# Another order for the first projection's matrix products, and three small loads on another DMA queue, in a two-layer encoder kernel

## The chip, the cores and the metric

The kernel runs on one core of a Trainium2 chip (trn2). The metric is the device time of one execution, in microseconds (us), taken as the median of several runs. The engines are called PE (TensorE: matrix products, transposes), DVE (VectorE), ACT (ScalarE), POOL (GpSimd) and SP (SyncE, which here only starts transfers). "ACTq" and "SPq" are the instruction queues of ACT and SP when they start a transfer.

## What is computed

The reference is a two-layer encoder on one sequence of 256 tokens and 1024 channels. Only the first steps of the first layer matter here:

```python
def _rmsnorm(x, g):
    x32 = x.astype(jnp.float32)
    inv = lax.rsqrt(jnp.mean(x32 * x32, axis=-1, keepdims=True) + EPS)
    return (x32 * inv).astype(x.dtype) * g

def _swiglu(h, w_in, w_out):
    gu = h @ w_in
    gate, up = jnp.split(gu, 2, axis=-1)
    return (jax.nn.silu(gate) * up) @ w_out

def reference(x, ...):
    for l in range(DEPTH):
        x = x + 0.5 * _swiglu(_rmsnorm(x, ffn1_norm[l]), ffn1_w_in[l], ffn1_w_out[l])
        # the mixer: p = h @ w_mix_in, spatial gating and windowed attention, @ w_mix_out
        x = x + 0.5 * _swiglu(_rmsnorm(x, ffn2_norm[l]), ffn2_w_in[l], ffn2_w_out[l])
    return x
```

`w_in` is 1024 x 5632 (gate and up halves of 2816 columns), `w_out` 2816 x 1024, all float32. `rel_bias` (32 x 8 numbers) becomes the attention's position bias, needed in the mixer.

## The kernel before, in words

**Products in three parts.** Every float32 operand is split into a rounded part "hi" (float32r) and the rest "lo" = original - hi. A product of two operands is the sum of three PE products: hi*hi, hi*lo and lo*hi. For weights ACT writes `w_hi` with a copy and DVE writes `w_lo` with a subtraction. For the input, PE transposes a token tile of 128 rows into PSUM (`TR`), DVE multiplies it with the norm's gain into `sc` (`take_xg`), ACT rounds that into `xT_hi` and DVE subtracts into `xT_lo`. The 1/rms of each token is applied later, to the result.

**Weights as a stream of units.** A unit is 128 x 2048 numbers (1 MB). SP loads units in their order of use into three buffers `raw`; `w_hi` and `w_lo` have six slots each. Unit n+3 is loaded when DVE has made `w_lo` of unit n (semaphore `lo_ready`). Position 0 and 1 of the first feed-forward block hold 256 gate and 256 up columns (chunk 0) for input channels 0-511 and 512-1023; positions 2 and 3 are chunk 1's gate and up columns, 4 is the 256 rows of `w_out` for chunk 0, 5 and 6 are chunk 2's, 7 is chunk 1's rows, and so on through 11 chunks. Units 0 and 1 come in two halves each (`load_first`), which ACT and DVE split half by half (`split_first`, `split_rest`), so that PE can start early.

**Order of work.** There is no scheduler: each engine's program is one list written out by hand, and semaphores hold an instruction back until what it needs is there. An engine works strictly in its own order. The opening of layer 0 goes like this:

- PE: 6 warm-up products, the transpose of the first norm's gains, transposes of token tile 0 (`transpose_x(0, 0, 0)`), 12 more warm-up products (`warm_up`, all on the identity matrix, their results unused). Then `ffn(0, 0)`: `enter(0, 0)` (12 products of tile 0 with unit 0), transposes of tile 1, `enter(0, 1)`, `enter(1, 0)`, `enter(1, 1)` (12 products each). `enter` waits for `xT_lo` of its half and calls `project`, which waits for the lower part of the unit's first half (`half_lo`) before any product, and for the whole unit (`split_ready`) before its second half. Each k tile then has its three products in a row (`products`, L1123, L1124, L1126).
- After that PE waits for `h_done`: the gated activation of tile 0 (`mul_rows`, DVE L782, on ACT's `silu_rows`, L513), then computes chunk 1's gate columns (`enter_T(1, 0, 0)`, L1186 and L1194), transposes the activations of both tiles (`transpose_h`, L1176), and goes on with `enter_T(1, 0, 1)`, `enter_T(1, 1, 0)`, which waits for `hT_lo` of tile 0 (L788), `other_rows()` (L1394 to L1398: it transposes the rest of the small parameter rows and waits for their loads, `rows_loaded` and `head_rows_loaded`), `enter_T(1, 1, 1)` and `leave(0, t)`.
- ACT: the halves of units 0 and 1, rounding of tile 0, two sums of squares (L551), rounding of tile 1 (`take_xT(0, 0, 1)`, L556). Then it starts three small loads (`rb`, L699; two sets of 16 rows of norm gains, L701), stores the two 1/rms vectors to DRAM (`store_inverse`, L562, which waits for POOL's result `inv_done`), splits unit 2, does `silu_rows` of tile 0, splits unit 3, `silu_rows` of tile 1, splits unit 4, reads the 1/rms back spread over partitions (L567), and rounds the transposed activations (`take_hT`, L535).
- DVE: the subtractions for units 0 and 1 between the input's, then `w_lo` of unit 2, `mul_rows` of tile 0, `w_lo` of unit 3, `mul_rows` of tile 1, `take_hT` (L788) for both tiles, `w_lo` of unit 4.
- POOL: 1/rms of both tiles (`inverse_rms`, L431 and L432), three loads of small rows (q and k gains, L446; `sgu_b`, L448), then the table `brow`, built from `rb` with 31 copies (L454), its store to DRAM (L459) and, spread over the next chunks, 8 loads of `bias` (L465).

## Time and profile before

| What | Value |
|---|---|
| median of 3 runs | 909.88 us (909.81 to 909.89) |
| the profiled execution | 909.78 us |
| its span in the profile | 908.0 us |
| PE busy | 901.9 us (99%) |
| PE weight loads | 767.2 us (84%) |
| DVE, ACT, POOL busy | 610.8, 483.0, 48.1 us |
| HBM traffic | 184 GB/s over the span |
| granted PE clock, every slice | 9 (90% or more) in tenths |

The profiled execution is 0.10 us under the median of the runs, and 1.8 us of it lie outside the profiled span. Times in rows are microseconds from the start of the span. A PE product is drawn until its result is out, so its length overlaps the next one; the step from one start to the next is what it takes from PE.

### The profile page before, as it was taken

To read this page: it belongs to the slowest core of one execution; us is meant where nothing else is said; L and a number is where in the kernel's file an instruction comes from. 1 tells how busy PE (TensorE), PEld (TensorE's weight loads), DVE (VectorE), ACT (ScalarE), POOL (GpSimd) and SP (SyncE) were. 2 spreads that over 40 slices of the span, in tenths; PEclk is the share of its full clock that TensorE was granted. 3 is DMA by queue.
4 is the path that set the end of the run, shared out by engine and by line. 5 is a ranking of instruction groups with operands and counts; after the bars stand their busy time and mean duration, and the time that the engine had idled before them with its cause. 6 is when DMAs were issued, how large, how long until landed. Compare 5 with 4: busy or idle time off the path is not lost.

```text
span 908.0 us, 13716 instructions
## 1 busy us (share of the span) xinstructions
PE 901.9 (99%) x4902; PEld 767.2 (84%) x4902; DVE 610.8 (67%) x791; ACT 483.0 (53%) x604; POOL 48.1 (5%) x105
## 2 busy tenths in 40 slices
PE   8999999999999999999999999999999999999998
PEld 7888888887788888888888888888877888888887
DVE  5576666687966765665776666666789567566564
ACT  6455455467845554544555545535678355454551
POOL 2200001012100000000010000000210100000000
PEclk9999999999999999999999999999999999999999
DMA  8776666654174656455547555554531656645531
GB/s 280 237 221 206 218 205 201 226 169 139 51 261 131 215 185 220 151 200 214 164 158 249 182 201 188 185 214 157 186 139 47 232 157 221 230 146 204 205 139 46
DMA packets 120909, 167.53 MB, mean 185 GB/s; under 512 B 7101, under 2 KB 100097, under 8 KB 120873
## 3 DMA queue, kind: packets, MB, share of 16 engines
q1 hardware_dynamic: 117536, 163.47, 53.2%
q0 software_dynamic: 1104, 2.90, 1.4%
q10 hardware_dynamic: 2232, 0.69, 0.4%
q8 instruction: 22, 0.36, 0.2%
q14 instruction: 15, 0.11, 0.0%
HBM read 165.71 MB, written 1.31 MB: 184 GB/s over the span
## 4 chain that ended last, share of the span: by engine, by line
PE 92%; DVE 5%; ACT 1%; DMA 1%; issue 1%; SPq 0%; ACTq 0%; DVEq 0%
PE TR L1186 16%; PE U L1186 16%; PE TR L1194 8%; PE U L1194 8%; PE C L1123 6%; PE C L1126 6%; PE C L1124 6%; PE D L1126 5%; PE D L1123 5%; PE D L1124 5%; PE U L1123 2%; PE U L1126 2%; PE U L1124 2%; DVE sc L982 1%; DVE w_lo L766 1%; PE TR L1163 1%
## 5 line engine op out<-in xcount | busy, mean ns | idle before, releaser
L766 DVE TENSOR_TENSOR w_lo<-raw,w_hi 128x2048 fp32r<-128x2048 f32 x150 | 340.1, 2289 | 109.2 <-ACT w_hi L494 109.1
L494 ACT ACTIVATE w_hi<-raw 128x2048 fp32r<-128x2048 f32 x150 | 282.2, 1905 | 20.3 <-DMA raw<-in_ffn_w_in_dram 12.9
L1186 PE MATMUL U<-xT,w_hi 128*128 128x512 f32 x640 | 167.4, 392 | 0.3 <-DVE small L782 0.3
L1186 PE MATMUL TR<-xT,w_hi 128*128 128x512 f32 x640 | 165.9, 391 | 0.0
L1186 PEld LDWEIGHTS TR<-xT,w_hi 128*128 128x128 f32 x640 | 119.2, 188 | 21.5
L1186 PEld LDWEIGHTS U<-xT,w_hi 128*128 128x128 f32 x640 | 115.1, 189 | 20.2 <-DVE small L782 0.7
L518 ACT ACTIVATE small<-U 128x512 f32<-128x512 f32 x40 | 23.9, 598 | 151.8 <-PE U L1186 151.7
L1194 PEld LDWEIGHTS U<-xT,w_lo 128*128 128x128 f32 x640 | 86.9, 189 | 6.5
L1194 PEld LDWEIGHTS TR<-xT,w_lo 128*128 128x128 f32 x640 | 87.6, 190 | 4.3
L1194 PE MATMUL TR<-xT,w_lo 128*128 128x256 f32 x640 | 89.4, 282 | 0.0
L1194 PE MATMUL U<-xT,w_lo 128*128 128x256 f32 x640 | 88.7, 281 | 0.0
L540 ACT ACTIVATE hT_hi<-small 128x256 fp32r<-128x256 f32 x80 | 33.1, 418 | 89.2 <-DVE small L812 89.2
L793 DVE TENSOR_TENSOR small<-U,small 128x512 f32<-128x512 f32 x40 | 27.6, 690 | 71.1 <-ACT small L518 70.9
L1123 PE MATMUL D<-w_hi,hT_hi 128*128 128x512 f32 x176 | 68.7, 390 | 0.0
L1124 PE MATMUL D<-w_lo,hT_hi 128*128 128x512 f32 x176 | 68.5, 389 | 0.0
L1123 PE MATMUL C<-w_hi,hT_hi 128*128 128x512 f32 x176 | 68.5, 389 | 0.0
L1124 PE MATMUL C<-w_lo,hT_hi 128*128 128x512 f32 x176 | 68.5, 389 | 0.0
L805 DVE TENSOR_TENSOR small<-TR,small 128x256 f32<-128x256 f32 x80 | 33.7, 421 | 43.0 <-ACT small L527 42.8
L531 ACT ACTIVATE small<-small 128x512 f32<-128x512 f32 x40 | 25.3, 632 | 67.8 <-DVE small L800 67.8
L1126 PE MATMUL D<-w_hi,hT_lo 128*128 128x512 f32 x176 | 55.5, 389 | 0.0
L1123 PE MATMUL U<-w_hi,xT 128*128 128x512 f32 (+1 forms) x144 | 54.8, 381 | 0.4 <-DVE xT L857 0.4
L1126 PE MATMUL C<-w_hi,hT_lo 128*128 128x512 f32 x176 | 54.2, 389 | 0.0
(140 smaller groups left out, 1110.8 us busy)
## 6 DMA issues: line engine op xcount, KB each, us to landing
raw<-in_ffn_w_in_dram SPq DMA_DIRECT2D x168, 512.0 KB, 4.7
raw<-in_ffn_w_out_dram SPq DMA_DIRECT2D x88, 512.0 KB, 4.1
raw<-in_w_mix_in_dram SPq DMA_DIRECT2D x28, 512.0 KB, 4.3
raw<-in_w_mix_out_dram SPq DMA_DIRECT2D x16, 512.0 KB, 3.7
raw<-in_ffn_w_in_dram SPq DMA_DIRECT2D x16, 256.0 KB, 4.4
bias<-bias_rows POOLq DMA_DIRECT2D x8, 192.0 KB, 5.4
xs<-in_x_dram SPq DMA_DIRECT2D x2, 512.0 KB, 4.9
out_dram<-xs SPq DMA_DIRECT2D x3, 256.0 KB, 2.1
```

What stands on the lines that cost most here:

```text
L494: act.activation(w_hi[:, p % SLOTS, :], raw[:, p % RAW, :], ACT.Copy).then_inc(hi_ready, 1)
L518: act.activation(gate, U_pair[:, :, S:2 * S], ACT.Copy).then_inc(gate_copied, 1)
L531: act.activation(gate, gate, ACT.Silu).then_inc(silu_done, 1)
L540: act.activation(hT_hi[:, c % 2, kk, :], h[:, kk, :], ACT.Copy).then_inc(hT_hi_done, 1)
L766: dve.tensor_tensor(w_lo[:, p % SLOTS, :], raw[:, p % RAW, :], w_hi[:, p % SLOTS, :].bitcast(F32), ALU.subtract).then_inc(lo_ready, 1)
L793: dve.tensor_tensor(gate, U_pair[:, :, 0:S], gate, ALU.add).then_inc(gate_added, 1)
L805: dve.tensor_tensor(h[:, kk, :], TR[kk][:, 0:S], h[:, kk, :], ALU.add).then_inc(up_added, 1)
L1123: pe.matmul(out_, x_hi, w_hi[:, slot, c], start=start, stop=False)
L1124: pe.matmul(out_, x_hi, w_lo[:, slot, c], start=False, stop=False)
L1126: last = pe.matmul(out_, x_lo, w_hi[:, slot, c], start=False, stop=stop)
L1186: last = pe.matmul(to, w_hi[:, slot, cols_of(k, kk)], xT[:, k, :, :], start=k == 0, stop=k == KT - 1)
L1194: last = pe.matmul(to[:, 0:S], w_lo[:, slot, cols_of(k, kk)], xT_hi[:, k, :], start=False, stop=False)
```

## The change

PE's first four groups of products in layer 0 are written out in a function of their own, `enter_first`. It waits for each part of the operands by itself and issues the products that need only that part: hi*hi as soon as the rounded parts are there, then hi*lo or lo*hi. Tile 0's transposes of the next tile stand after 16 of its products instead of 12. The products are the same 48, added into the same PSUM banks. All other projections, and the same place in layer 1, are as before. The loads of `rel_bias` and of 2 x 16 rows of norm gains leave ACT's list and stand in POOL's, after the two `inverse_rms` and ahead of POOL's own three small loads.

```diff
@@ POOL @@
             inverse_rms(0, 0, 0)
             inverse_rms(0, 0, 1)
+            with nc.allow_non_contiguous_dma(reason="256 numbers, once"):
+                pool.dma_start(rb[:, :], rel_bias.rearrange("b h -> h b")).then_inc(rb_loaded, 16)
+            for r0, v in ((16, mix_norm), (32, ffn2_norm)):
+                pool.dma_start(rows[r0:r0 + 2 * KT, :], v.rearrange("l (k p) -> (l k) p", p=P)).then_inc(rows_loaded, 16)
             for r0, v in ((48, q_norm), (50, k_norm)):
@@ ACT @@
             for L in range(DEPTH):
                 take_xT(L, 0, 1)
-                if L == 0:
-                    with nc.allow_non_contiguous_dma(reason="256 numbers, once"):
-                        act.dma_start(rb[:, :], rel_bias.rearrange("b h -> h b")).then_inc(rb_loaded, 16)
-                    for r0, v in ((16, mix_norm), (32, ffn2_norm)):
-                        act.dma_start(rows[r0:r0 + 2 * KT, :], v.rearrange("l (k p) -> (l k) p", p=P)).then_inc(rows_loaded, 16)
                 ffn(L, 0, [POS_KV, POS_Q, POS_Q + 1])
@@ PE @@
+            def enter_first():
+
+                def product(t, k, w_of):
+                    kk = k % 4
+                    return pe.matmul(U[t][:, :], xT_hi[:, k, t * P:(t + 1) * P], w_of[:, k // 4, kk * 512:(kk + 1) * 512],
+                                     start=k == 0 and w_of is w_hi, stop=False)
...
+                pe.wait_ge(half_hi, 1)
+                pe.wait_ge(xT_hi_done, n_tran(0, 0, 0, 0))
+                high_high(0, (0, 1))
+                pe.wait_ge(half_lo, 1)
+                high_low(0, (0, 1))
+                pe.wait_ge(xT_lo_done, n_tran(0, 0, 0, 0))
+                low_high(0, (0, 1))
+                pe.wait_ge(hi_ready, n_unit(0, 0))
+                high_high(0, (2, 3))
+                low_high(0, (2, 3))
+                split_ready(0, 0)
+                high_low(0, (2, 3))
+                pe.wait_ge(half_hi, 2)
+                pe.wait_ge(xT_hi_done, n_tran(0, 0, 0, 1))
+                high_high(0, (4, 5))
+                pe.wait_ge(xT_lo_done, n_tran(0, 0, 0, 1))
+                low_high(0, (4, 5))
+                pe.wait_ge(x_loaded[1], 16)
+                transpose_x(0, 0, 1)
+                pe.wait_ge(half_lo, 2)
+                high_low(0, (4, 5))
+                pe.wait_ge(hi_ready, n_unit(0, 1))
+                high_high(0, (6, 7))
+                split_ready(0, 1)
+                high_low(0, (6, 7))
+                low_high(0, (6, 7), True).then_inc(gu_ready, 1)
+                for u in range(2):
+                    ks = range(4 * u, 4 * u + 4)
+                    pe.wait_ge(xT_hi_done, n_tran(0, 0, 1, u))
+                    high_high(1, ks)
+                    high_low(1, ks)
+                    pe.wait_ge(xT_lo_done, n_tran(0, 0, 1, u))
+                    low_high(1, ks, True).then_inc(units_used, 1)
...
-                enter(0, 0)
-
-                if f == 1:
-                    pe.wait_ge(x_new, n_x_new(L, 1, 1, 1))
+                if L == 0 and f == 0:
+                    enter_first()
                 else:
-                    pe.wait_ge(x_loaded[1], 16)
-                    pe.wait_ge(x_new, n_x_new(L, -1, 1, 1))
-                pe.wait_ge(xg_done, n_tran(L, 2 * f, 0, 1))
-                transpose_x(L, 2 * f, 1)
-                enter(0, 1)
-                enter(1, 0)
-                enter(1, 1)
+                    enter(0, 0)
+
+                    pe.wait_ge(x_new, n_x_new(L, 2 * f - 1, 1, 1))
+                    pe.wait_ge(xg_done, n_tran(L, 2 * f, 0, 1))
+                    transpose_x(L, 2 * f, 1)
+                    enter(0, 1)
+                    enter(1, 0)
+                    enter(1, 1)
```

PE's list from the second warm-up to the transposes of tile 1, before the change. In brackets stand the semaphores that an instruction waits for; L1123 is hi*hi, L1124 the product with `w_lo`, L1126 the one with `xT_lo`. A row that only repeats the one ahead of it is left out here and in the next list.

```order
L1391 MATMUL C1<-ident 128x128 x12
L1123 MATMUL U<-w_hi,xT 128x512 [waits half_lo,xT_lo_done]
L1124 MATMUL U<-w_lo,xT 128x512
L1126 MATMUL U<-w_hi,xT 128x512
...
L1123 MATMUL U<-w_hi,xT 128x512 [waits lo_ready]
...
L1163 MATMUL TR<-ident,xs 128x128 [waits xg_done,x_new,x_loaded1]
```

The same place after the change (L1169 is now a product with `xT_hi`, L1183 the one with `xT_lo`).

```order
L1446 MATMUL C1<-ident 128x128 x12
L1169 MATMUL U<-w_hi,xT 128x512 [waits xT_hi_done,half_hi]
L1169 MATMUL U<-w_lo,xT 128x512 [waits half_lo]
L1183 MATMUL U<-w_hi,xT 128x512 [waits xT_lo_done]
L1169 MATMUL U<-w_hi,xT 128x512 [waits hi_ready]
L1183 MATMUL U<-w_hi,xT 128x512 x2
L1169 MATMUL U<-w_lo,xT 128x512 [waits lo_ready]
L1169 MATMUL U<-w_hi,xT 128x512 [waits xT_hi_done,half_hi]
L1183 MATMUL U<-w_hi,xT 128x512 [waits xT_lo_done]
L1162 MATMUL TR<-ident,xs 128x128 [waits x_loaded1]
```

The first product waited for both lower parts; now it waits for the two rounded parts, and the lower parts are waited for one by one, with two products behind each wait.

ACT's list from the rounding of tile 1 to `silu_rows` of tile 0, before:

```order
L556 ACTIVATE xT<-sc 128x4x128 [waits xg_done] x2
L699 DMA rb<-in_rel_bias_dram 8x32x1
L701 DMA wsT<-in_mix_norm_dram 16x128
L701 DMA wsT<-in_ffn_norm_dram 16x128
L562 DMA inv_rows<-inv 128x1 [waits inv_done]
L562 DMA inv_rows<-inv 128x1
L494 ACTIVATE w_hi<-raw 128x2048 [waits units_used,unit_loaded2]
L513 ACT_TABLE_LOAD [waits inv_done]
L513 ACTIVATE small<-U,inv 128x256 [waits gu_ready]
```

and after:

```order
L560 ACTIVATE xT<-sc 128x4x128 [waits xg_done] x2
L566 DMA inv_rows<-inv 128x1 [waits inv_done]
L566 DMA inv_rows<-inv 128x1
L498 ACTIVATE w_hi<-raw 128x2048 [waits units_used,unit_loaded2]
L517 ACT_TABLE_LOAD [waits inv_done]
L517 ACTIVATE small<-U,inv 128x256 [waits gu_ready]
```

The three loads are gone from ACT's list, and the stores of the 1/rms follow the rounding at once. POOL's list at the place where they now stand:

```order
L431 TENSOR_SCALAR mean<-ms 128x1 [waits ms_done]
L432 TENSOR_TENSOR inv<-mean,mhalf 128x1 [waits pool_step]
L446 DMA rb<-in_rel_bias_dram 8x32x1
L448 DMA wsT<-in_mix_norm_dram 16x128
L448 DMA wsT<-in_ffn_norm_dram 16x128
L450 DMA wsT<-in_q_norm_dram 2x2x64
L450 DMA wsT<-in_k_norm_dram 2x2x64
L452 DMA wsT<-in_sgu_b_dram 8x128
L454 MEMSET brow 8x511
L458 COPY brow<-rb 8x38 [waits rb_loaded,pool_step]
```

The q, k and `sgu_b` loads stood directly behind `inverse_rms` and now have the three moved ones ahead of them.

## Rows read from the trace of the kernel before

**Rows 1.** The page, busy time of the engines over the whole span.

```profile
PE 901.9 (99%) x4902; PEld 767.2 (84%) x4902; DVE 610.8 (67%) x791; ACT 483.0 (53%) x604; POOL 48.1 (5%) x105
```

**Rows 2.** Waits of PE, whole span: us in total, times, longest.

```profile
PE C L1391 <- POOL mhalf L426: 1.7, 1, 1.7
PE U L1123 <- DVE xT L857: 0.4, 1, 0.4
PE TR L1176 <- DVE small L782: 0.3, 1, 0.3
PE U L1186 <- DVE small L782: 0.3, 1, 0.3
```

**Rows 3.** Timeline of PE, 4 to 31.3 us: start, length, instruction, [idle before <- releaser].

```profile
5.66 2.84 PE L1391 MATMUL C<-ident 128*128 128x128 f32 x24
8.93 0.50 PE L1123 MATMUL U<-w_hi,xT 128*128 128x512 f32 x1 [0.42 <-DVE xT L857]
...
11.83 1.09 PE L1163 MATMUL TR<-ident,xs 128*128 128x128 f32 x8
12.67 0.47 PE L1123 MATMUL U<-w_hi,xT 128*128 128x512 f32 x1
...
20.74 0.39 PE L1126 MATMUL U<-w_hi,xT 128*128 128x512 f32 x1
21.42 0.50 PE L1186 MATMUL U<-xT,w_hi 128*128 128x512 f32 x1 [0.30 <-DVE small L782]
...
28.10 0.39 PE L1186 MATMUL TR<-xT,w_hi 128*128 128x512 f32 x1
...
30.99 0.27 PE L1398 MATMUL C<-ident,wsT 60*128 60x60 f32 x1
```

**Rows 4.** Timeline of DVE, 4 to 32 us, same columns.

```profile
11.91 1.22 DVE L776 TENSOR_TENSOR w_lo<-raw,w_hi 128x1024 fp32r<-128x1024 f32 x1
...
18.74 2.29 DVE L766 TENSOR_TENSOR w_lo<-raw,w_hi 128x2048 fp32r<-128x2048 f32 x1 [3.02 <-ACT w_hi L494]
20.95 0.42 DVE L782 SCALAR_TENSOR_TENSOR small<-U,small 128x256 f32<-128x256 f32 x1
...
27.10 0.76 DVE L788 TENSOR_TENSOR hT_lo<-TR,hT_hi 128x256 fp32r<-128x256 f32 x2 [2.13 <-ACT hT_hi L535]
```

**Rows 5.** Timeline of ACT, 5 to 45 us, same columns.

```profile
6.92 1.14 ACT L556 ACTIVATE xT<-sc 128x512 fp32r<-128x512 f32 x2
...
13.77 1.23 ACT L556 ACTIVATE xT<-sc 128x512 fp32r<-128x512 f32 x2
14.37 0.54 ACTq L699 DMA_DIRECT2D rb<-in_rel_bias_dram  x1
...
15.77 0.92 ACTq L562 DMA_DIRECT2D inv_rows<-inv  x2
16.79 1.92 ACT L494 ACTIVATE w_hi<-raw 128x2048 fp32r<-128x2048 f32 x1 [1.79 <-issue]
...
24.78 1.91 ACT L494 ACTIVATE w_hi<-raw 128x2048 fp32r<-128x2048 f32 x1 [2.12 <-DMA raw<-in_ffn_w_out_dram]
...
26.68 0.66 ACT L535 ACTIVATE hT_hi<-TR 128x256 fp32r<-128x256 f32 x2
```

**Rows 6.** Timeline of POOL, 14 to 41 us, same columns.

```profile
14.31 0.55 POOL L432 TENSOR_TENSOR inv<-mean,mhalf 128x1 f32<-128x1 f32 x1
14.81 0.77 POOL L446 DMA_DIRECT2D wsT<-in_q_norm_dram  x1
...
16.16 0.56 POOL L448 DMA_DIRECT2D wsT<-in_sgu_b_dram  x1
```

**Rows 7.** DMA issues in a window: count, KB each, median us from issue to landing.

```profile
raw<-in_ffn_w_in_dram SPq DMA_DIRECT2D x2, 512.0 KB, 6.5
...
raw<-in_ffn_w_out_dram SPq DMA_DIRECT2D x2, 512.0 KB, 8.5
...
wsT<-in_sgu_b_dram POOLq DMA_DIRECT2D x1, 4.0 KB, 9.0
```

More of the change, by code:

```diff
@@ L1164, in transpose_x, with high_high, high_low, low_high @@
                     last.then_inc(xT_psum, 1)
+            def enter_first():
[3 more added lines that the diff above has]
+                                     start=k == 0 and w_of is w_hi, stop=False)
+                def high_high(t, ks):
+                    for k in ks:
+                        product(t, k, w_hi)
+                def high_low(t, ks):
+                    for k in ks:
+                        last = product(t, k, w_lo)
+                    return last
+                def low_high(t, ks, stop=False):
+                    for k in ks:
+                        last = pe.matmul(U[t][:, :], xT_lo[:, k, t * P:(t + 1) * P],
+                                         w_hi[:, k // 4, (k % 4) * 512:(k % 4 + 1) * 512],
+                                         start=False, stop=stop and k == KT - 1)
+                    return last
+                pe.wait_ge(half_hi, 1)
[31 more added lines that the diff above has]
+                    low_high(1, ks, True).then_inc(units_used, 1)
```

## The prediction

> **What bounds the kernel now.** I read the page first: PE is busy 901.9 of 908.0 us [rows 1], so what the end can move by is what PE waits, plus what its own work costs. The list of PE's waits for the whole span comes next, and it has four entries only [rows 2]: 1.7 us before the first warm-up, and three of 0.4, 0.3 and 0.3 us, all of which stand in the first 26 us. Behind them PE works without a wait to the end. Two things follow. A microsecond won in the opening stays won, for nothing later would take it up. And the ceiling is low: the change touches no later place. Then I read the timelines of the four engines side by side in the opening.
>
> PE's warm-up products end near 8.35 (24 of them from 5.66, each step about 0.12 us), yet the first real product starts at 8.93, released by DVE's `xT_lo` [rows 3]. From 12.67 to 20.74 stand 36 products, 35 steps and so (8.07)/35 = 0.23 us each; the transposes of tile 1 take 12.67 - 11.83 = 0.84 us. PE is through with the 48 products at 20.74 + 0.23 = 20.97, and then the next product starts at 21.42, released by DVE's `mul_rows` [rows 3].
>
> That second wait hangs on a chain that starts on ACT. Its rounding of tile 1 ends at 15.00; it starts the first small load at 14.37 and the stores of 1/rms at 15.77, for 0.92 us, so that unit 2's rounding begins only at 16.79, behind an idle time of 1.79 us whose releaser is "issue" [rows 5]. DVE's `w_lo` of unit 2 begins at 18.74 (idle 3.02 us for ACT) and takes 2.29 us, `mul_rows` stands behind it from 20.95 to 21.37 [rows 4], and PE starts at 21.42. So the three loads are on the path to 21.42, though ACT is busy only half of the span.
>
> **The change, part by part.**
>
> *PE's new order.* Rounded parts: `xT_hi` of the first half is there by 6.92 + 0.57 = 7.49, before the warm-ups end at 8.35 [rows 3, 5]. DVE makes the first half of `w_lo` ahead of `xT_lo`, whose end released PE at 8.93; so the products with `w_lo`, wanted two products later at 8.4 + 0.46 = 8.86, wait 0.07 us at most, and those with `xT_lo`, wanted at 9.3, not at all. So PE should run from about 8.4 without a stall: 48 x 0.23 + 0.84 + about 0.2 for the first start = 12.1, done at 8.35 + 12.1 = 20.4 instead of 20.97. The second unit's last subtraction ends at 13.13 [rows 4], and its two products with `w_lo` come as numbers 21 and 22, at 8.4 + 20 x 0.23 + 0.84 = 13.8, so that wait is covered, with 0.7 us over. Transposes of tile 1 move from 11.83 to 8.4 + 16 x 0.23 = 12.1, which costs nothing, since DVE takes their results only when it is done with `w_lo` at 13.13. PE gains 0.57 us here. By itself this is worth nothing: the next thing PE waits for is `mul_rows` at 21.37, which does not use PE's last products, so PE would arrive earlier and wait longer.
>
> *The loads off ACT.* They fill 15.77 - 14.37 = 1.40 us of ACT's queue [rows 5]. Not all of it comes back, as the stores behind them wait for POOL's second 1/rms, which ends at 14.31 + 0.55 = 14.86 [rows 6]. So the stores start at 14.93 instead of 15.77: gain 0.84 us. Unit 2's rounding then starts at 15.95; its `w_lo` at 17.90, `mul_rows` ends at 20.53, and PE goes on at 20.58 instead of 21.42. PE itself is ready at 20.4, just in time. Units 2 and 3 must be in `raw` by then: unit 3 was issued up to 11.27 and landed after 6.5 us in the median [rows 7], at 17.8, and it is wanted at 20.39 - 0.84 = 19.55. The second short wait (0.3 us, for `mul_rows` of tile 1) hangs on the same chain and moves with it. Without the new order, PE would come at 20.97 and the loads alone would give 21.37 - 20.97 = 0.3 to 0.4 us. So the parts belong together: order 0, loads about 0.4, both 0.84.
>
> *The next wait.* PE comes to `enter_T(1, 1, 0)` at 28.10 - 0.84 = 27.26 [rows 3]. It needs `hT_lo` of tile 0, whose subtraction ran from 27.10, 0.38 us for the first of the two, so until 27.48 [rows 4]; that was after ACT's `take_hT` at 26.68, which stood behind unit 4's rounding, and this began at 24.78, released by the landing of `w_out` [rows 5]. The landing does not move with ACT. If it stays, PE waits 27.53 - 27.26 = 0.27 us, plus 0.1 us for starting afresh (the first product after the stall, at 8.93, is 0.50 us long and that at 20.74 0.39 [rows 3]), and the gain is 0.5 us. If it comes only 0.3 us sooner, the gain is the whole 0.84 us. `w_out`'s two halves took 8.5 us in the median from issues at 13.2 and 13.7 [rows 7], hence one of them took about 11 us to 24.7. I take it that the landing comes somewhat earlier, since the 1/rms stores start earlier and no longer have `rb`'s 256 numbers ahead of them on their queue; no row shows this, so the two ends are 0.84 and, if it comes 0.5 us later, 0.
>
> *The loads on POOL.* An issue there takes 0.56 to 0.77 us [rows 6]: three add 1.7 to 2.3 us. `sgu_b`, the last, was issued at 16.16 and landed 9.0 us later, at 25.2 [rows 7]; now 27.5 at most, with the same 9.0 us. PE wants it at 30.99 - 0.84 = 30.15 in `other_rows()` [rows 3]: 2.6 us of cover. The price of an issue with 256 separate numbers is not in the trace on POOL; ACT took 0.54 us for it [rows 5]. It lies between 0.5 us and the 2.6 us of cover more than the rest before it costs anything. `brow` and `bias` are wanted chunks later, so their delay costs nothing. POOL's own next duty, the 1/rms of the next block, comes far later.
>
> Sum: -0.84 from both parts, 0 to +0.35 from the landing of `w_out`; I take -0.8. On the profiled execution that is 909.78 - 0.8 = 908.98, and the median lies 0.10 above it: **909.1 us**.
>
> **The rivals.**
>
> *A, the `w_out` landing takes the place of the removed wait.* As above, -0.5 us if it stays, less if it comes later: 909.4 to 909.9. For it: ACT's row at 24.78 already names this transfer as releaser after 2.12 us idle. Against: only 0.3 us earlier are enough. The Trainium skill speaks for it ("DMA: Bandwidth & Descriptors", Queues, rings and completion order): each DMA engine serves the queue rows that have work in turn, so loads on POOL's row beside those of SP and ACT would take turns from the weights. By it the landing would come later and the gain would go towards 0. No row here shows which queue an engine served.
>
> *B, slower: the small rows come late and PE stalls in `other_rows()`.* POOL's issue at 14.81 ran beside a DVE subtraction and took 0.77 us, the one at 16.16 with DVE idle took 0.56 us [rows 6]. If DVE can hold POOL for a whole subtraction, the last issues meet `w_lo` of unit 2 (17.90 to 20.2) and that of unit 3 (21.5 to 23.8), and `sgu_b` is issued at 23.8 and lands 9.0 us later at 32.8, where PE wanted it at 30.15: 2.65 us of stall and 0.1 for starting afresh against 0.84 of gain, 909.88 + 1.91 = 911.8 us. It decides from an issue later than 30.15 - 9.0 = 21.15. Against it: 0.2 us is all that the two rows differ by. The Trainium skill has the rule ("SBUF — State Buffer", SBUF: two separate sides): while DVE works in its two-port mode POOL cannot write descriptors, and a POOL transfer of about 620 ns took about 3100 ns. The trace bears it out only in the 0.2 us.
>
> *C, more than forecast.* Were the stores not held by POOL's 1/rms, the chain would gain the 1.40 us, and PE, ready at 20.4, would use 1.0 of it: 908.8 us.
>
> *D, nothing.* ACT's issue goes as late as before, for a reason the profile does not show, or `w_out` lands 0.5 us later: 909.8 us.
>
> **How the numbers follow.** Forecast (gain 0.7 to 0.9) 0.45; A 0.30; C 0.07; D 0.12; B 0.05; something unforeseen of over 2 us gain 0.01. The range 908.6 to 910.0 holds the forecast, A, C and D, all but B and the tails. A difference of 0.2% is 1.8 us, about what a measurement of this kernel can tell from no change. All cases but B lie within it: same 0.93, slower 0.05, faster 0.02.
>
> **What would show it.** First product near 8.4 and no DVE releaser before it; products in steps of 0.23 us until the transposes near 12.1; PE done with 48 products near 20.4; stores of 1/rms issued from 14.93; unit 2's rounding at 15.95; PE's next product at 20.58. Then at 27.3 either no idle time (forecast) or one of 0.3 us with DVE's `hT_lo` as releaser (A). An idle time on PE before L1398's successor with a DMA as releaser would be B. I am wrong if PE has a new wait anywhere behind 31 us, or if the stores start as late as 15.8.

## The result, and the profile after

| | before | after |
|---|---|---|
| median of 22 runs each | 909.88 us | 910.77 us |
| lowest to highest | 909.62 to 910.60 | 909.50 to 913.14 |
| profiled execution, its span | 909.78, 908.0 us | 910.46, 908.7 us |

The ratio is 1.0014 (95% interval 1.0008 to 1.0020): slower by 0.14%, 0.9 us in the medians, where I forecast 909.1 us. Both the sign and the range were wrong. The change's runs fall into two groups: 14 from 909.50 to 910.96 us with a mean granted clock of 1.000, and 8 from 912.40 to 913.14 us with 0.998. The profiled execution is from the first group. The 14 runs alone have a median of 910.4 us, 0.5 over before; the rest of the 0.9 comes from the runs with 0.998.

First the page's busy times of the changed kernel and its list of PE's waits (us in total, times, longest), against [rows 1, 2].

```profile
PE 901.9 (99%) x4902; PEld 767.3 (84%) x4902; DVE 611.2 (67%) x791; ACT 482.8 (53%) x604; POOL 49.8 (5%) x108
```

```profile
PE C L1446 <- POOL mhalf L426: 1.7, 1, 1.7
PE TR L1242 <- DVE hT_lo L787: 1.4, 1, 1.4
PE TR L1232 <- DVE small L781: 0.3, 1, 0.3
```

PE's own work is the same to a tenth. The wait for `xT_lo` and that for `mul_rows` of tile 0 are gone, as forecast; in their place stands one of 1.4 us for `hT_lo`. PE's timeline in the opening, against [rows 3]:

```profile
5.85 2.84 PE L1446 MATMUL C<-ident 128*128 128x128 f32 x24
8.45 0.71 PE L1169 MATMUL U<-w_hi,xT 128*128 128x512 f32 x2
...
12.18 1.03 PE L1162 MATMUL TR<-ident,xs 128*128 128x128 f32 x8
...
19.43 1.07 PE L1183 MATMUL U<-w_hi,xT 128*128 128x512 f32 x4
20.40 0.50 PE L1242 MATMUL U<-xT,w_hi 128*128 128x512 f32 x1
...
28.64 0.50 PE L1242 MATMUL TR<-xT,w_hi 128*128 128x512 f32 x1 [1.42 <-DVE hT_lo L787]
...
31.64 0.27 PE L1453 MATMUL C<-ident,wsT 60*128 60x60 f32 x1
```

At 20.40 the change leads by 21.42 - 20.40 = 1.02 us. At 28.64 it trails by 28.64 - 28.10 = 0.54, at L1453 by 31.64 - 30.99 = 0.65, and at the end of the span by 0.7. From L1453 to the end both kernels take 877.0 to 877.1 us (908.7 - 31.64, 908.0 - 30.99), so this one instruction's start tells what a kernel is worth; I use it below. All is won and lost ahead of 28.64. ACT's timeline says by what, against [rows 5]:

```profile
13.69 1.14 ACT L560 ACTIVATE xT<-sc 128x512 fp32r<-128x512 f32 x2
14.84 0.83 ACTq L566 DMA_DIRECT2D inv_rows<-inv  x2
15.77 1.92 ACT L498 ACTIVATE w_hi<-raw 128x2048 fp32r<-128x2048 f32 x1 [0.95 <-POOL inv L432]
...
25.95 1.91 ACT L498 ACTIVATE w_hi<-raw 128x2048 fp32r<-128x2048 f32 x1 [4.31 <-DMA raw<-in_ffn_w_out_dram]
...
27.77 0.64 ACT L539 ACTIVATE hT_hi<-TR 128x256 fp32r<-128x256 f32 x2
```

ACT is 1.0 us ahead at its unit 2 (15.77 against 16.79) and has nothing to do from 21.6: it waits 4.31 us for `w_out`, which it sees landed at 25.95, not at 24.78. `take_hT` then runs at 27.77 (26.68 before), DVE's subtraction at 28.16 (27.10 before, [rows 4]), and PE, which arrives at 28.64 - 1.42 = 27.22, stands still. `w_out` was issued no later (SP's timeline: from 12.97, before from 13.2). What did the DMA engines do meanwhile? The busy times by stretch; of the last three columns the first is PE's granted clock, the second the DMA engines' busy share, the third GB/s.

```profile
20.00:22.00 2.00, 2.00 (x14) 1.59 (x13) 1.04 (x3) 1.64 (x2) 0.00 (x0) 1.00 0.57 27
22.00:24.00 2.00, 1.71 (x10) 1.16 (x8) 1.94 (x2) 0.00 (x0) 0.00 (x0) 1.00 0.08 3
24.00:26.00 2.00, 2.00 (x14) 1.87 (x15) 0.00 (x0) 0.05 (x1) 0.12 (x1) 1.00 0.26 44
```

From 22 to 24 us they moved 3 GB/s. In the trace's list of packets the last 4 KB packet of `w_out` ends at 20.24, and the last one of ACT's stores at 20.35. Each half of a load raises its semaphore in sixteen steps, one for each part. Of the second half of `w_out` three parts were reported by 21.27 and the other thirteen between 23.87 and 25.92; before the change 14 were reported by 21.42, one at 22.28 and one at 24.75. So the report came up to 5.7 us after the last packet. The loads behind it were held up too: the pair of `w_in` halves that SP started at 20.26 and 20.85 had only landed at 32.19. POOL's side, against [rows 6, 7], first its timeline and then the DMA issues (median us to landing):

```profile
14.25 0.56 POOL L432 TENSOR_TENSOR inv<-mean,mhalf 128x1 f32<-128x1 f32 x1
14.75 0.90 POOL L446 DMA_DIRECT2D rb<-in_rel_bias_dram  x1
...
17.81 0.55 POOL L452 DMA_DIRECT2D wsT<-in_sgu_b_dram  x1
...
25.88 6.11 POOL L458 COPY brow<-rb 8x38 f32<-8x38 f32 x31 [7.01 <-DMA rb<-in_rel_bias_dram]
```

```profile
inv_rows<-inv ACTq DMA_DIRECT2D x2, 0.5 KB, 11.0
rb<-in_rel_bias_dram POOLq DMA_DIRECT2D x1, 1.0 KB, 11.0
...
wsT<-in_sgu_b_dram POOLq DMA_DIRECT2D x1, 4.0 KB, 9.9
```

`sgu_b` landed at 17.81 + 9.9 = 27.7, wanted at 31.64: no cost. POOL sees `rb` at 25.88 as ACT sees `w_out` at 25.95: several transfers of different queues are reported at about the same time.

### The profile page after: what moved, and what is told of

It is laid out like the page before. It is cut to its first block, busy times and chain, and to the rows that moved or that the text cites. A ratio compares the mean times of both kernels' runs of the same rounds, so it can differ in the third digit from the quotient of the medians.

```text
span 908.7 us, 13713 instructions
## 1 busy us (share of the span) xinstructions
PE 901.9 (99%) x4902; PEld 767.3 (84%) x4902; DVE 611.2 (67%) x791; ACT 482.8 (53%) x604; POOL 49.8 (5%) x108
## 4 chain that ended last, share of the span: by engine, by line
PE 92%; DVE 5%; DMA 2%; ACT 1%; issue 0%; SPq 0%; DVEq 0%
PE TR L1242 16%; PE U L1242 16%; PE TR L1250 8%; PE U L1250 8%; PE C L1122 6%; PE C L1125 6%; PE C L1123 6%; PE D L1125 5%; PE D L1122 5%; PE D L1123 5%; PE U L1122 2%; PE U L1125 2%; PE U L1123 2%; DVE sc L981 1%; DMA raw<-in_ffn_w_out_dram 1%; DVE w_lo L765 1%
## 5 line engine op out<-in xcount | busy, mean ns | idle before, releaser
L792 DVE TENSOR_TENSOR small<-U,small 128x512 f32<-128x512 f32 x40 | 27.7, 691 | 73.3 <-ACT small L522 73.0
L1123 PE MATMUL D<-w_lo,hT_hi 128*128 128x512 f32 x176 | 68.5, 389 | 0.0
L1123 PE MATMUL C<-w_lo,hT_hi 128*128 128x512 f32 x176 | 68.5, 389 | 0.0
L1122 PE MATMUL U<-w_hi,xT 128*128 128x512 f32 (+1 forms) x128 | 48.4, 378 | 0.0
```

Of the source, the lines that this page charges most:

```text
L792: dve.tensor_tensor(gate, U_pair[:, :, 0:S], gate, ALU.add).then_inc(gate_added, 1)
L1122: pe.matmul(out_, x_hi, w_hi[:, slot, c], start=start, stop=False)
L1123: pe.matmul(out_, x_hi, w_lo[:, slot, c], start=False, stop=False)
```

## The experiments

Three things could hold back `w_out`'s completion. **Theory 1:** `rb`'s 256 single numbers, now on POOL's queue beside `w_out`. **Theory 2:** the two 1/rms stores of 128 single numbers each (`inv_rows`), which start 0.9 us earlier than before and so meet more of `w_out`. **Theory 3:** POOL's loads in flight, whatever they are made of. The kernel before, run again beside each set, took 909.91, 910.00, 909.92 and 909.92 us. "Landing" is the start of ACT's rounding of `w_out`; where ACT came later than the data, it is an upper end.

**The parts apart.** `e1_order_only`: the three loads go back to ACT.

```diff
-                pool.dma_start(rb[:, :], ...)      # and the two loads of rows
+                    act.dma_start(rb[:, :], ...)   # behind take_xT(0, 0, 1), as before
```

> The new order of the products alone; the three loads stay on ACT's list. The trace of the change shows PE's new order as forecast and then a wait of 1.42 us at 27.2 for hT_lo, behind a landing of w_out at 25.9 instead of 24.7. All theories on that landing put its cause in the small transfers, so here it stays near 24.7: PE is ready at 20.4 and waits for mul_rows until 21.4 as before, and the time is that of before, 909.9 us within 0.15. If the new order itself moved the landing, the time would be over 910.3 us.

Measured: 910.43 us (910.27 to 910.80, 11 runs), ratio 1.0003 [0.9994, 1.0013], 0.5 more than expected. PE in its trace:

```profile
4.78 1.97 PE L1163 MATMUL TR<-ident,xs 128*128 128x128 f32 x8
...
12.97 1.03 PE L1163 MATMUL TR<-ident,xs 128*128 128x128 f32 x8
```

The first transposes took 1.97 us, in the change 1.23 and before 1.09. The trace's record of the granted clock says why: it shows full speed, the 2.4 GHz level, from 6.69 us on here, from 5.11 in the change and from 4.62 before. The 128x128 products ahead of that moment start 0.21 us apart, those behind it 0.11. (The view by stretches prints 1.00 even ahead of it, because the record starts only there.) So the transposes of tile 1 come at 12.97, and DVE, which I had counted as busy to 13.13, has waited 0.39 us for them. To see whether this is chance, the same kernel once more:

> The kernel with the new order alone once more, for a second trace. Its first took 910.43 us in the median, 0.5 over before, and its trace shows PE's clock at 1.2 GHz until 6.69 us (4.62 before), so that warm-ups, products and tile 1's transposes come 0.8 us late and DVE waits 0.39 us for them at 13.6, ACT 0.56 at 14.3. Theory W (the new order has no slack against late warm-ups): where the clock rises near 5 us, DVE does not wait and the time is 909.9; where it rises past 6 us it is 910.4. Theory P (the transposes after 16 products instead of 12 delay DVE in any case): DVE waits at 13 us whatever the clock does.

It gave 910.04 us in one run, with full speed from 6.21, the first transposes at 1.76 us and no wait on DVE: between the theories, and it settles nothing. (e13 below has full speed from 6.23 and DVE's wait again, 0.35 us.) `e9_transposes_after_14` takes the cover back instead: order only, tile 1's transposes two products earlier.

```diff
                 high_high(0, (4, 5))
-                pe.wait_ge(xT_lo_done, n_tran(0, 0, 0, 1))
-                low_high(0, (4, 5))
                 pe.wait_ge(x_loaded[1], 16)
                 transpose_x(0, 0, 1)
+                pe.wait_ge(xT_lo_done, n_tran(0, 0, 0, 1))
+                low_high(0, (4, 5))
```

> The new order alone, with tile 1's transposes two products earlier (after 14 instead of 16), just when x has landed (11.7 to 11.8 us). Theory P or W: the transposes, and with them DVE's and ACT's rounding of tile 1 and everything behind it up to mul_rows, come up to 0.45 us earlier than in the new order alone, so 910.0 to 910.1 us instead of 910.43. If the 0.5 us have another cause: 910.4 us still.

Measured: 909.98 us (909.66 to 910.32), 1.0001 [0.9992, 1.0010], as expected. The intervals of the two ratios overlap, but only one of the 11 runs here is above the lowest of e1. The reading that fits is that "later transposes cost nothing" had too little slack: where PE's clock rises late, the order-only kernel pays, about 0.45 us between the two medians. It isn't shown closer than that, for in e9's own trace the clock was up at 4.77. I didn't try this edit on the full change.

`e2_loads_only`: the loads on POOL, PE's order as before (`enter_first` taken out).

> The loads on POOL alone; the products in their old order. Theories 1 to 3 (the small transfers delay w_out's landing): landing near 25.9, PE waits for hT_lo until 28.6, end as in the full change, 910.4 to 910.9 us, with some runs 2 us slower. Theory 4 (the landing only varied by chance in the profiled execution): about 0.3 us faster than before, 909.6 us.

Measured: 912.94 us (910.44 to 914.55), 1.0027 [1.0018, 1.0036]; 7 of 11 runs had a mean granted clock of 0.998 or less, which puts the median 2 us over what I expected. So the loads' part carries the loss. ACT and PE in its trace:

```profile
14.86 0.84 ACTq L566 DMA_DIRECT2D inv_rows<-inv  x2
...
27.24 1.91 ACT L498 ACTIVATE w_hi<-raw 128x2048 fp32r<-128x2048 f32 x1 [5.57 <-DMA raw<-in_ffn_w_out_dram]
```

```profile
29.93 0.50 PE L1185 MATMUL TR<-xT,w_hi 128*128 128x512 f32 x1 [2.67 <-DVE hT_lo L787]
```

With the stores as early as in the change, PE stalls 2.67 us.

**Theories 1 and 3.** `e3_rb_in_8_pieces`: the full change, `rb` read in 8 runs of 128 bytes instead of 256 single numbers (which leaves wrong entries in the bias table).

```diff
-                pool.dma_start(rb[:, :], rel_bias.rearrange("b h -> h b")).then_inc(rb_loaded, 16)
+                pool.dma_start(rb[:, :], rel_bias.rearrange("(a b) h -> a (b h)", a=NH)).then_inc(rb_loaded, 16)
```

> The full change, but rel_bias is read in 8 contiguous runs of 128 bytes instead of 256 single numbers, so that the bias table holds wrong entries. Theory 1 (the 256 single-number writes of rb, now on a queue of their own beside the 256 of the 1/rms stores, hold up the completions): w_out lands at 24.7 or earlier, PE's wait at 27.2 shrinks to 0.3 us or nothing, time 909.0 to 909.4 us. Theory 2 (the 1/rms stores, started 0.9 us earlier, stand ahead of w_out's last completions) and theory 3 (three more loads on POOL's queue, whatever their shape): no change, 910.4 to 910.9 us.

Measured: 911.19 us (910.05 to 912.95), 1.0014 [1.0005, 1.0023], the same as the change; landing at 26.73. Theory 1 falls. The profiled execution is one with clock 0.998 and shows where the other two microseconds come from. PE, and the stretches around the stall:

```profile
29.43 0.72 PE L1242 MATMUL TR<-xT,w_hi 128*128 128x512 f32 x1 [2.20 <-DVE hT_lo L787]
...
33.96 0.27 PE L1453 MATMUL C<-ident,wsT 60*128 60x60 f32 x1
```

```profile
26.00:28.00 2.00, 1.23 (x6) 0.68 (x4) 0.00 (x0) 1.27 (x1) 1.70 (x13) 1.00 0.69 55
28.00:30.00 2.00, 0.57 (x2) 0.48 (x3) 1.05 (x3) 1.67 (x4) 0.40 (x1) 0.88 0.48 128
30.00:32.00 2.00, 2.00 (x10) 1.99 (x9) 2.00 (x2) 0.00 (x0) 0.00 (x0) 0.50 1.07 379
32.00:34.00 2.00, 2.00 (x8) 1.28 (x6) 0.50 (x1) 0.00 (x0) 0.00 (x0) 0.76 1.01 347
```

PE stood still for 2.20 us up to 29.43; then its granted clock fell to 0.50, the 1.2 GHz level, and the same work up to L1453 took 33.96 - 29.43 = 4.53 us where the change's trace has 31.64 - 28.64 = 3.00. That is 1.5 us more, beside the stall itself, and 911.0 - 34.0 = 877.0 us remain as always.

`e5_small_loads_first`: all six small loads of POOL right behind the constants, so that none is in flight with `w_out`.

```diff
             pool.memset(mhalf[:, :], -0.5).then_inc(consts_ready, 1)
+            # rb, mix_norm, ffn2_norm, q_norm, k_norm, sgu_b
...
             inverse_rms(0, 0, 1)
-            # rb, mix_norm, ffn2_norm, q_norm, k_norm, sgu_b
```

> The full change, but all six small loads stand first in POOL's list, right after the constants, so that none is in flight when w_out lands; the 1/rms stores stay where the change has them. Theory 2 (the stores of 256 single numbers to DRAM hold up w_out's completion): the landing stays at 25 to 27 us, time 910.3 to 912.5 us. Theory 3 (the loads on POOL's queue hold it up): landing by 22.3, PE does not wait at 27.2, time 909.0 us or, with the chain on ACT shortened no further, 908.9.

Measured: 911.33 us (910.97 to 913.46), 1.0015 [1.0006, 1.0024]. ACT:

```profile
10.09 1.06 ACT L504 ACTIVATE w_hi<-raw 128x1024 fp32r<-128x1024 f32 x1 [7.55 <-DMA raw<-in_ffn_w_in_dram]
...
19.05 0.83 ACTq L566 DMA_DIRECT2D inv_rows<-inv  x2
...
27.45 1.92 ACT L498 ACTIVATE w_hi<-raw 128x2048 fp32r<-128x2048 f32 x1 [1.54 <-DMA raw<-in_ffn_w_out_dram]
```

The small loads, single numbers among them, now meet the first weights, and those are seen at 10.09 instead of 5.71; PE waits 3.2 us there. `w_out`, issued 4.4 us later than in the change (17.35), lands 10.1 us after its issue, against 13.0 in the change and 8.6 in e4 below; 15 of the 16 parts of its second half were reported by 22.78. So a delay is there without POOL's loads, but a smaller one, and the upset opening makes the comparison a weak one. It takes e12 to decide on theory 3.

**Theory 2, the stores.** `e4_inv_store_late`: the full change; in the first block the stores stand behind the rounding of `w_out`, and the reading back behind it.

```diff
-                store_inverse(L, f)
+                if not first:                  # first: layer 0, block 0
+                    store_inverse(L, f)
                 split(L, pos_in(f, 1, 0))
...
                 split(L, pos_out(f, 0))
-                spread_inverse(L, f)
+                if first:
+                    store_inverse(L, f)
+                else:
+                    spread_inverse(L, f)
...
                 copy_up(L, f, 1, 1)
+                if first:
+                    spread_inverse(L, f)
```

> The full change, but in the first block of layer 0 the two stores of 1/rms (256 single numbers to DRAM) start only after unit 4's rounding, and the spreading load correspondingly later. Theory 2: w_out lands by 22.3, where 15 of its 16 parts were in the run before, so PE does not wait at 27.2; time 909.0 us. ACT's rounding of unit 2 also comes 0.9 us earlier, but PE is ready only at 20.4, which gives 0.2 us more at most. Theory 1: rb's 256 numbers still delay the landing to 24.5 or later, 909.3 to 910.5 us. The late spreading load could make DVE's scale_gate wait near 42, which PE does not feel until 50.

Measured: **908.22 us** (907.83 to 909.27), 0.9982 [0.9973, 0.9991], better than expected. ACT:

```profile
14.93 1.90 ACT L498 ACTIVATE w_hi<-raw 128x2048 fp32r<-128x2048 f32 x1
...
21.87 1.92 ACT L498 ACTIVATE w_hi<-raw 128x2048 fp32r<-128x2048 f32 x1 [0.84 <-DMA raw<-in_ffn_w_out_dram]
21.87 0.83 ACTq L566 DMA_DIRECT2D inv_rows<-inv  x2
```

`w_out` lands at 21.87 instead of 25.95, with all six loads on POOL still there: theory 2 holds. PE's only wait left is the one before the warm-up. What I had underrated is the second effect: the stores' issue (0.83 us) leaves ACT's path too, unit 2's rounding begins at 14.93, and the 0.3 us for `mul_rows` of tile 1 goes as well.

The slow stretch has moved as well. The stretches of e4's trace, same columns as before:

```profile
22.00:24.00 2.00, 2.00 (x13) 1.70 (x12) 1.08 (x2) 2.00 (x3) 2.00 (x11) 1.00 1.01 330
24.00:26.00 2.00, 2.00 (x14) 1.78 (x13) 1.91 (x3) 0.33 (x2) 2.00 (x8) 1.00 1.30 51
```

The stores' packets now end at 24.36, and from there to 30 us the DMA engines move 51 to 58 GB/s, with two `w_in` halves started at 22.99 and 23.55 in the queue, which have landed only at 34.90. The pair ahead of them, started at 19.40 and 19.99, had landed at 24.72. In e8 below, with its stores at 21.97, the stretches from 26 to 34 us are the slow ones (35 to 73 GB/s). So the stores still hold up what is in flight behind them, for some 6 to 8 us; here that is a load that nothing waits for.

Is it then the change or the stores? `e6_before_inv_store_late` has the same edit on the kernel before.

> The kernel before, with nothing of the change, but with the first block's 1/rms stores moved behind unit 4's rounding. It tells what the change is worth when the landing is out of the way. The stores' 0.9 us leave ACT's path, so mul_rows of tile 0 ends near 20.5 and PE, ready at 20.97 in the old order, does not wait: 0.4 us, and 0.3 us for the second wait: 909.1 to 909.3 us by theory 2. The kernel with the change and the late stores took 908.22 us, so the change would be worth about 0.9 us there. If the late stores were worth nothing without the change: 909.9 us.

Measured: 908.98 us (908.80 to 910.08), 0.9989 [0.9981, 0.9998]. The kernel before paid for the early stores too, 0.9 to 1.0 us, and once they are late the change is worth 908.98 - 908.22 = 0.76 us, close to the 0.84 that I had worked out. (The intervals of the two ratios overlap; 9 of e4's 11 runs lie below the lowest of e6.) And its parts? `e11_order_and_late_stores` is e4 with the three loads back on ACT.

> New order and late stores, the three small loads left on ACT. With late stores alone 908.98 us, with the full change and late stores 908.22 us. In the trace with late stores alone mul_rows of tile 0 ends at 20.50 and PE's old order ends at 21.0: PE bounds. So the order should bring what there was (PE ready near 20.3, mul_rows at 20.5): 908.4 to 908.5 us; moving the loads on top is worth 0.2 us only. If the moved loads carry the 0.76 us: 908.9 us.

Measured: 909.68 us (908.97 to 910.65), 0.9995 [0.9986, 1.0004]; expected 1.2 us less. PE's waits in its trace:

```profile
PE C L1454 <- POOL mhalf L426: 1.7, 1, 1.7
PE U L1177 <- ACT xT L556: 0.7, 1, 0.7
PE TR L1240 <- DVE small L789: 0.3, 1, 0.3
PE U L1250 <- DVE small L789: 0.3, 1, 0.3
```

With the loads on ACT the waits for `mul_rows` are back; the 0.7 us is a first weight that came late in this execution, the slowest of the 11. ACT takes that weight up at 7.82 us against 6.03 in e6's trace, so I compare the rows less 1.8: PE takes up chunk 1 at 20.5 (22.33 less 1.8) against 20.97 in e6, then waits for `mul_rows` of tile 1 and gets past it at 24.3 (26.11 less 1.8) against 24.35. So the second `mul_rows`, which my expectation left out, takes the gain back. Even the lowest of 11 runs, 908.97, is no better than the median of late stores alone, 908.98: the order alone is worth nothing here either. Why the median is 0.7 us worse is open; the late first weight is seen in one trace only.

What about the stores does it? `e7_stores_after_silu`: the full change with the stores one step later in ACT's list, behind `silu_rows` of tile 0, and the reading back as late as in e4.

> The full change with the 1/rms stores at another time: started behind silu_rows of tile 0, near 18.3 us, instead of 14.84 or 21.87, the spreading load late as in the run with late stores. Theory 2 with the time of the stores as what counts (their numbers must not come before w_out's last parts, which move until 20): landing 21 to 23, 908.2 to 908.9 us. If any store that starts before the landing delays it: landing 24 or later, 909.5 to 911 us.

Measured: 911.26 us (909.27 to 914.32, 12 runs), 1.0014 [1.0003, 1.0025]. ACT:

```profile
15.02 1.90 ACT L498 ACTIVATE w_hi<-raw 128x2048 fp32r<-128x2048 f32 x1
15.17 0.84 ACTq L566 DMA_DIRECT2D inv_rows<-inv  x2
...
25.64 1.91 ACT L498 ACTIVATE w_hi<-raw 128x2048 fp32r<-128x2048 f32 x1 [4.57 <-DMA raw<-in_ffn_w_out_dram]
```

The stores did not move: they start at 15.17, beside the rounding listed ahead of them and before the `silu_rows` that should have held them. So "an engine works strictly in its own order", as I wrote ahead of the prediction, doesn't hold for a transfer in ACT's list, and the run can't say what a start at 18 us does. It does say two other things: the late reading back is not what helps e4, and an issue hidden beside a rounding isn't enough.

`e8_single_number_reads`: e4, and at the stores' old place two loads of 128 single numbers each into a spare tile.

```diff
+                    act.wait_ge(inv_done, 2)
+                    with nc.allow_non_contiguous_dma(reason="256 numbers, once"):
+                        for t in range(2):
+                            act.dma_start(spare[:, t:t + 1], x_tiles[t][:, 0:1]).then_inc(spare_loaded, 16)
```

> The full change with late stores, plus, at 14.84 us where the stores stood, two loads of 128 single numbers from DRAM into a spare SBUF column: the same counts and sizes, the other direction. If writing single numbers to DRAM is the cause, w_out lands by 22.3 and the time is 908.2 to 908.6 us. If any 256 single numbers at that time delay the landing: 25 us or later, 910.3 us or more.

Measured: 908.98 us (908.67 to 910.74), 0.9990 [0.9981, 0.9998]. ACT:

```profile
14.90 0.84 ACTq L596 DMA_DIRECT2D spare<-in_x_dram  x2
...
21.96 1.92 ACT L500 ACTIVATE w_hi<-raw 128x2048 fp32r<-128x2048 f32 x1 [0.23 <-DMA raw<-in_ffn_w_out_dram]
```

As many pieces, at the same time and on the same queue, but read from DRAM: `w_out` lands at 21.96, unharmed. It needs the writes to DRAM. The 0.76 us above e4 fit the issue's being back on ACT's path (0.84 us); I haven't shown them apart.

`e10_stores_behind_w_out`: the full change; the stores go out from SP, in the queue of `w_out` and behind it, as early as in the change.

```diff
                 chunk(0)
+                if L == 0 and f == 0:
+                    sp.wait_ge(inv_done, 2)
+                    for t in range(2):
+                        sp.dma_start(inv_rows[0, t, :].unsqueeze(1), inv[:, t:t + 1]).then_inc(inv_stored, 16)
...
-                store_inverse(L, f)            # ACT
+                if not first:                  # first: layer 0, block 0
+                    store_inverse(L, f)
```

> The full change with the 1/rms stores in SP's list, right behind the load of w_out (unit 4), waiting for POOL's result at 14.8 us; the spreading load late as before. The single-number stores start as early as in the change (14.9), but in SP's own queue, behind w_out's pieces in it. If what counts is that the small writes come ahead of w_out's last pieces on the same DMA engine, w_out lands by 22.3 and the time is 908.2 us. If what counts is only when they start or that they overlap with its completion: landing 25 us or later, 910 us or more.

Measured: **908.22 us** (907.87 to 909.40), 0.9984 [0.9975, 0.9993]. SP, then ACT:

```profile
13.12 0.82 SPq L324 DMA_DIRECT2D raw<-in_ffn_w_out_dram  x2
14.68 0.80 SPq L382 DMA_DIRECT2D inv_rows<-inv  x2
```

```profile
20.84 1.92 ACT L502 ACTIVATE w_hi<-raw 128x2048 fp32r<-128x2048 f32 x1
```

The same writes begin at 14.68, earlier than the change's 14.84, and the last part of `w_out` is reported at 20.81: ACT doesn't wait at all. So what counts is not the number of these stores or the time of their start, but whether they can get ahead of `w_out`'s last pieces on the DMA engines. From another queue they can; behind it in its own they can't. The loads behind the stores pay here too: the four `w_in` halves started from 19.27 landed after 11.6 us in the median (10.5 in the change, 7.5 in e4), and PE waits for none of them.

The Trainium skill has the mechanism ("DMA: Bandwidth & Descriptors", Queues, rings and completion order): a transfer's semaphore is raised by a strongly ordered write, which lands only after every earlier write of that DMA engine, across its queues. The traces agree: idle DMA engines with `w_out` unreported, `rb` and `w_out` reported at 25.88 and 25.95, and the pair e4 and e10. The price here is 25.95 against 21.87, some 4 us. No row shows the writes of one DMA engine in their order, so the rule is the reading that fits and isn't shown by itself; and it speaks of reports, not of the slow loads behind the stores, for which these runs give no cause.

**Why later than before?** So far all kernels with stores at 14.8 to 15.2 us also had the three loads on POOL. `e12_pool_loads_after_unit3` keeps the early stores and starts POOL's loads only after `mul_rows` of tile 0. `e13_stores_at_15_6` keeps POOL's loads and holds the stores with a semaphore until DVE's `xT_lo` of tile 1.

```diff
             inverse_rms(0, 0, 1)
+            pool.wait_ge(h_done, n_ffn(0, 0, 0, 0))           # e12 alone
...
                 act.wait_ge(inv_done, n_inv(L, 2 * f, 1))
+                if L == 0 and f == 0:                          # e13 alone
+                    act.wait_ge(xT_lo_done, n_tran(0, 0, 1, 1))
```

> The full change, but POOL starts its six small loads only after the gated activation of tile 0 (about 20.4 us), when the data of w_out is through. The 1/rms stores start at 14.84 as in the change. If the start of the stores alone decides how late w_out is reported: landing at 25.6 to 27.2 us (12.3 to 14.0 us after its issue), 910.2 to 911.5 us. If POOL's loads in flight add to what the stores do: landing no later than 25.0 (11.8 us after its issue, as in the kernels that leave the loads on ScalarE), 909.2 to 909.9 us, and no runs with a lower clock. If sgu_b, issued from 23.5, comes after 31 us, a wait at the rows' transpose adds to either.

> The same kernel as e12 once more, for the scatter of the landing: each theory expects the landing that it expects of e12, within 0.7 us of it.

> The full change, but the 1/rms stores wait in addition for the second tile's last lower part (DVE, ends at 15.6), so that they start as late as in the kernel before, with POOL's loads left at 14.75. If the start of the stores decides: landing at 24.3 to 24.9 us (11.1 to 11.6 us after the issue) and 909.7 to 910.0 us. If POOL's loads in flight add to it: landing at 25.6 or later and 910.3 us or more.

> The same kernel as e13 once more, for the scatter of the landing: each theory expects the landing that it expects of e13, within 0.7 us of it.

e12: 912.52 us (910.94 to 914.94, 6 runs), 1.0029 [1.0016, 1.0041], and 913.83 in the repeat. ACT, then the stretch from 20 us:

```profile
15.09 0.83 ACTq L567 DMA_DIRECT2D inv_rows<-inv  x2
...
26.49 1.91 ACT L499 ACTIVATE w_hi<-raw 128x2048 fp32r<-128x2048 f32 x1 [4.59 <-DMA raw<-in_ffn_w_out_dram]
```

```profile
20.00:22.00 2.00, 2.00 (x14) 1.52 (x13) 1.04 (x3) 1.89 (x2) 1.09 (x2) 1.00 0.06 10
```

The landing is at 26.49 (25.98 in the repeat), with none of POOL's loads started before 20.91, and between 20 and 22 us the DMA engines are idle but for 6%. Theory 3 falls. The rest of the time is the small rows: issued up to 22.8, they make PE wait 1.4 us at the rows' transpose, rival B's place by another cause.

e13: 909.95 us (909.68 to 910.70, 10 runs), 1.0001 [0.9991, 1.0010], and 909.80 in the repeat. POOL's loads beside `w_out` cost nothing once the stores start as late as before. Its landings are 25.54 and 24.65, the first 0.6 later than expected. In the time it doesn't show: unit 2's rounding starts at 17.11 again, PE waits 0.7 and 0.3 us for `mul_rows`, and so comes late enough to find `hT_lo` ready.

`w_out`'s issue lies between 12.97 and 13.49 in these kernels, so times are best counted from it:

| stores, us after `w_out`'s issue | kernels | `w_out` reported, us after its issue | of the 16 parts of its second half, reported later than 10 us |
|---|---|---|---|
| 1.61, 1.62 | e3, e2 | 13.5, 14.0 | 16, 16 |
| 1.77, 1.84, 1.87, 1.92 | e12, e7, change, e12b | 13.2, 12.3, 13.0, 12.7 | 13, 8, 13, 9 |
| 2.55, 2.56, 2.59, 2.60 | before, e9, e13b, e1b | 11.6, 11.2, 11.4, 11.4 | 1, 2, 4, 1 |
| 3.03, 3.04 | e1, e13 | 7.4, 12.4 | 0, 3 |
| 8 and more | e4, e6, e8 | 8.6, 8.3, 8.6 | 0, 0, 0 |

(In e1 and e6 ACT came later than the report; there the time is that of the last part.) The earlier the stores get in, the more parts of `w_out` are reported late and the later the last of them, with e13 as the one whose last part doesn't fit, and e5 (1.70, 10.1) aside. One late part is enough to hold the load: that is why the last column falls more evenly than the third. That is how 0.9 us won on ACT became 1.2 us lost on the landing.

## Why the prediction was wrong

- **What bounds the kernel**: right. PE's waits and nothing else moved, and all of it before 31 us.
- **PE's new order**: right to 0.1 us. First product at 8.45 (8.4), no wait for `xT_lo`, transposes at 12.18 (12.1), next product at 20.40 (20.4 to 20.58). "By itself this is worth nothing" holds in e9, and in e11 beside e6. Its number of 0.12 us for a step of the warm-up is 0.11 in the trace.
- **"Costs nothing, since DVE takes their results only when it is done with `w_lo` at 13.13"**: true in the change's own trace, but with a cover that a late rise of PE's clock uses up: in e1 DVE waits 0.39 us, and the order-only kernel is about 0.45 us slower than e9. I gave this slack no number.
- **The loads off ACT, 0.84 us**: right. Stores at 14.84 (14.93), unit 2 at 15.77 (15.95), limited by POOL's 1/rms as I said; with the landing out of the way the change brings 0.76 us.
- **The loads on POOL**: right. 0.50 to 0.90 us each, `sgu_b` landed at 27.7 (27.5 forecast), wanted at 31.64. Rival B falls: the issue at 17.81 took 0.55 us although DVE's `w_lo` ran from 17.72. The 0.77 us that I laid to DVE looks like the price of POOL's first transfer: the `q` load takes 0.77 us where it is the first (before, e1, e9) but 0.59 as the fourth in the change, with DVE idle, and 0.60 as the fourth in e12, beside a subtraction. The rule of the two-port mode from the Trainium skill ("SBUF — State Buffer", SBUF: two separate sides) that I named for B isn't seen in any of these issues.
- **The next wait: this step failed.** I had written "The landing does not move with ACT" and then "I take it that the landing comes somewhat earlier, since the 1/rms stores start earlier and no longer have `rb`'s 256 numbers ahead of them on their queue." I treated the stores as riders that only delay what follows them on their own queue. They delay the load that runs beside them, and the more the earlier they start. I had put the term at 0 to +0.35 us, with an outer end of 0.5 us later; it was 1.17 us later in the profiled execution, and at 25.6 to 27.2 over the kernels with early stores. The stall came out at 1.42 us, so the term measured 1.42 + 0.11 = 1.53 us against the 0.35 that was its upper end in the sum. In span time: a lead of 28.10 - 27.22 = 0.88 us when PE arrives, 1.42 for the stall, 0.11 for starting afresh, which makes +0.65 at L1453.
- **Rival A** had the place and the releaser right (DVE's `hT_lo` at 27.3 behind `w_out`), but not the cause that I gave for a later landing: POOL's loads beside the weights cost nothing (e12, e13). And I bounded it by "the gain goes towards 0". Nothing excluded a loss: a landing that another queue can delay by 1 us can be delayed by 2. (C's sum is off by a tenth: a gain of 1.0 gives 908.9 us, not 908.8.)
- **What no case had**: a stall of 1.4 us can cost more than itself. In 8 of 22 runs the change shows the clock of 0.998 and 2 us more. e3's trace shows in what place; that the change's own 8 runs lose it at the same place is inferred, since none of them was profiled.

Left open: what sets a landing to within a microsecond (e13's two differ by 0.9, counted from the issue by 1.0); why only some executions with a stall lose clock; what sets the moment from which PE's clock is at full speed (4.62 to 7.29 us in these traces); and why the loads behind the stores are slow for 6 to 8 us.

## What to carry to other kernels

Before moving work off an engine, list the transfers that this engine will now start earlier, and what big load is in flight at that moment on any queue: here the four-byte stores to DRAM held the report of a 1 MB load by 4 us, 1.2 of them because they came 0.9 us earlier than before, and turned a gain of 0.8 us into a loss of 0.9. Put such stores behind the load in its own queue, or after its landing; with that the same change gives 908.22 us, 1.7 us (0.18% and 0.16%) better than before. Of these, 0.9 to 1.0 us come from the stores' place alone (e6) and 0.76 from the change. The loads behind the stores stay slow for some microseconds wherever the stores stand, so choose a place where nothing waits for those loads. And judge a landing by the bytes as well as by the semaphore: where the DMA engines are all but idle with transfers in their queues, look for what is ahead of them, not only at the late load itself.

## What the runs showed of the hardware that I had not expected

- A completion can trail its last packet by microseconds: packets until 20.24, 3 GB/s between 22 and 24 us, landing at 25.95; 6% busy from 20 to 22 us, landing at 26.49 (e12). Two stores of 128 four-byte numbers are enough; two reads of the same shape do nothing (21.96).
- Behind such stores the DMA engines move little although loads are queued: 3 to 52 GB/s from 20 to 28 us in the change, 51 to 58 from 24 to 30 in e4, 31 to 68 from 20 to 28 in e10.
- ACT's queue starts a transfer ahead of the work listed before it: in e7 at 15.17, while the rounding from 15.02 ran, and before the `silu_rows` listed ahead of it. A place in ACT's list is no time for a transfer; a semaphore is.
- After a stall of 2.20 us (e3) PE's granted clock went to 0.50, the 1.2 GHz level; the three stretches from 28 to 34 us read 0.88, 0.50 and 0.76, and 1.5 us were lost. In e5 the 3.2 us wait for the first weights was followed by 0.50 in the stretch from 12 to 14 us. After the profiled 1.42 us it stayed at 1.00, the 2.4 GHz level. At the start of an execution full speed came between 4.62 us (before) and 7.29 (e12b) after about the same warm-up products.
- POOL's issue of 256 single numbers took 0.90 us (0.54 on ACT), the others in the change 0.50 to 0.59 us, DVE busy or not. Part of the 0.90 is being first: with `rb` in 8 pieces (e3) it took 0.75.
